# One inverse product a step in the chunked WKV recurrence

## What is computed

```python
def step(S, inp):
    r_t, w_t, k_t, v_t, kk_t, a_t = inp
    sa = jnp.einsum('bhvk,bhk->bhv', S, kk_t)
    S = (S * w_t[:, :, None, :]
         - sa[..., None] * (kk_t * a_t)[:, :, None, :]
         + v_t[..., None] * k_t[:, :, None, :])
    y = jnp.einsum('bhvk,bhk->bhv', S, r_t)
    return S, y
```

## Time and profile before

| | |
|---|---|
| runs, us | 2166.88, 2166.91, 2168.07, median 2166.91 |
| span of the profiled execution, us | 2162.8 |
| outside the span, against the median, us | 4.1 |
| PE busy in the span | 98% |
| DVE, ACT, POOL busy | 68%, 49%, 4% |
| recurrence, from step 0 to the first matmul of the next weight product | 1467.3 to 1563.9 us |
| mean use of the 16 DMA engines by the main queue | 55.8% |

### The profile page before, as it was taken

How to read it: one execution, slowest core, us unless ns; L and a number is a source line. 1 busy time by engine, 2 the same in 40 slices (tenths; PEclk the granted TensorE clock), 3 DMA queues, 4 the chain that set the end, 5 groups by cost and what they waited for, 6 DMA issues and landing times.

```text
span 2162.8 us, 36139 instructions
## 1 busy us (share of the span) xinstructions
PE 2128.1 (98%) x13990; PEld 1808.1 (84%) x13990; DVE 1466.9 (68%) x2083; ACT 1063.6 (49%) x1516; POOL 85.8 (4%) x75
## 2 busy tenths in 40 slices
PE   9999999999999999999899999999899999999998
PEld 7888878888888888888788888887788888888886
DVE  6556568885478855786795599884776544567656
ACT  5444455444444433444644766544434534456543
POOL 0800000000000000000000000001211000000000
PEclk9999999999999999999999999999999999999999
DMA  9654545555656556555465656653454555654553
GB/s 299 202 165 157 172 160 185 190 186 189 198 185 190 187 187 199 187 180 177 150 203 167 196 183 179 206 160 86 129 174 142 185 185 195 186 155 146 173 197 117
DMA packets 398856, 384.43 MB, mean 178 GB/s; under 512 B 43660, under 2 KB 395460, under 8 KB 397764
## 3 DMA queue, kind: packets, MB, share of 16 engines
q1 hardware_dynamic: 398728, 382.66, 55.8%
HBM read 375.73 MB, written 6.87 MB: 177 GB/s over the span
## 4 chain that ended last, share of the span: by engine, by line
PE 89%; DVE 7%; issue 2%; ACT 1%; DMA 1%; POOL 0%; SPq 0%; DVEq 0%; ACTq 0%; POOLq 0%
PE acc L894 35%; PE acc L897 17%; PE acc L1020 5%; PE acc L1022 5%; PE acc L1021 5%; PE acc L931 3%; PE acc L986 2%; PE acc L987 2%; PE acc L988 2%; PE aux L1319 2%; PE acc L934 1%; DVE w_lo L3001 1%; PE acc L1619 1%; PE acc L1620 1%; PE acc L1621 1%
## 5 line engine op out<-in xcount | busy, mean ns | idle before, releaser
L2448 DVE TENSOR_TENSOR w_lo<-raw_w,w_hi 128x1024 fp32r<-128x1024 f32 (+1 forms) x570 | 683.5, 1224 | 438.3 <-ACT w_hi L1692 437.5
L1692 ACT ACTIVATE w_hi<-raw_w 128x1024 fp32r<-128x1024 f32 (+1 forms) x570 | 586.3, 1045 | 706.0 <-PE acc L897 413.0
L894 PE MATMUL acc<-h,w_hi 128*128 128x512 f32 x1664 | 525.8, 397 | 0.0
L897 PEld LDWEIGHTS acc<-h,w_lo 128*128 128x128 f32 x1664 | 312.6, 188 | 73.8
L897 PE MATMUL acc<-h,w_lo 128*128 128x256 f32 x1664 | 327.0, 278 | 0.0
L894 PEld LDWEIGHTS acc<-h,w_hi 128*128 128x128 f32 x1664 | 254.7, 189 | 1.0
L894 PE MATMUL acc<-x_split,w_hi 128*128 128x512 f32 x704 | 225.1, 401 | 0.0
L894 PE MATMUL acc<-xs_b,w_hi 128*128 128x512 f32 x512 | 162.0, 398 | 1.0 <-DVE w_lo L3001 0.9
L897 PEld LDWEIGHTS acc<-x_split,w_lo 128*128 128x128 f32 x704 | 132.2, 188 | 31.2
L3001 DVE TENSOR_TENSOR w_lo<-raw_w,w_hi 128x1024 fp32r<-128x1024 f32 x96 | 116.8, 1219 | 42.1 <-ACT w_hi L2165 41.2
L894 PE MATMUL acc<-xs_a,w_hi 128*128 128x512 f32 x448 | 142.3, 399 | 0.7 <-DVE w_lo L3001 0.7
(11 more groups left out here) (459 smaller groups left out, 3223.5 us busy)
## 6 DMA issues: line engine op xcount, KB each, us to landing
raw_w<-in_w_up SPq DMA_DIRECT2D x172, 512.0 KB, 3.5
raw_w<-in_a_w_in SPq DMA_DIRECT2D x124, 512.0 KB, 3.9
raw_w<-in_w_in SPq DMA_DIRECT2D x64, 512.0 KB, 3.9
raw_w<-in_w_down SPq DMA_DIRECT2D x64, 512.0 KB, 3.5
raw_w<-in_b_w_qg SPq DMA_DIRECT2D x64, 512.0 KB, 3.7
raw_w<-in_w_o SPq DMA_DIRECT2D x32, 512.0 KB, 3.5
raw_w<-in_a_w_out SPq DMA_DIRECT2D x32, 512.0 KB, 3.5
raw_w<-in_w_k_shared SPq DMA_DIRECT2D x32, 512.0 KB, 3.3
```

The source lines that it names most:

```text
L894: pe.matmul(ACC[2 * b + f], WHI[:, q if hi is None else hi, k, f * P:(f + 1) * P], op[:, kt, :, :].rearrange("p h t -> p (h t)"), start=fi ...
L897: mm = pe.matmul(ACC[2 * b + f][:, 0:T], WLO[:, slot, k, f * P:(f + 1) * P], op[:, kt, 0, :], start=False, stop=last)
L1692: act.activation(WHI[:, u % 4, 0:ku, :], RAWW[:, u, 0:ku, :], ACT.Copy).then_inc(hi_made, 1)
L2448: dve.tensor_tensor(WLO[:, u, 0:ku, :], RAWW[:, u, 0:ku, :], WHI[:, u % 4, 0:ku, :].bitcast(F32), ALU.subtract)\
```

## The change

For all heads and chunks the corners are now made by PE in two blocks of 128 small products (32 x 32 tiles, 32 columns each), `corners_halfway` in step 0 and `corners` in step 1. For this:

- `t_scratch` becomes a full 64 x 64 layout. Two DMAs write zeros in its off-diagonal quarters (`blank_corners`, issued behind unit 88), two write the diagonal inverses. All four write runs of 32 values (128 bytes), 4096 runs each. 
- ACT turns the left diagonal inverses around (`left_turned`, behind unit 92), one DMA stores them, 8 DMAs of 1024 runs of 128 bytes load left and right factors, 4 load the cross blocks.
- ACT and DVE copy one half of each block of 128 products. SP stores the corners of groups 1 to 3 (3 DMAs of 1024 runs) and only then issues the bonus loads (`spread_bonus`, 2 MB), which before stood ahead of step 0.
- `load_t` is one DMA (512 runs of 256 bytes), plus the two cross loads in steps 0 to 3.

Steps 0 to 3 keep two inverse products. Steps 4 to 15 (`whole_step`) have one inverse product and no w product, no `US` copy and no add on DVE. Their order on PE is by tile shape: 64 x 64 (x_second, state times r, beta_pairs, u), then 128 x 64 (turn_k, turn_v, state product, y second term, turn_beta), then 64 x 64 (k_pairs of the step after next, x_first of the next). The state has two buffers (S and S_ODD), and y and state sums change banks from step to step. The core of the diff, with parts of SP's, PE's, ACT's and DVE's queues:

```diff
             def load_t(n):
                 g, c = STEPS[n]
                 m = n % 3
-                src = t_dram.rearrange("(f c h) b s t -> c h b s f t", c=NCH, h=2)
-                for hh in range(2):
-                    for b in range(2):
-                        at = 64 * hh + H * b
-                        sp.dma_start(TB[at:at + H, m, :, H * b:H * b + H], src[c, hh, b, :, 4 * g:4 * g + 4, :])\
-                          .then_inc(t_loaded[m], 16)
-                for e in range(2):
-                    sp.dma_start(CRS[64 * (1 - e):64 * (1 - e) + H, m, :, H:], cross_dram[g, c, e]).then_inc(t_loaded[m], 16)
+                src = t_dram.rearrange("(g i c h) s t -> g c (h s) i t", g=4, c=NCH, h=2)
+                sp.dma_start(TB[:, m, :, :], src[g, c]).then_inc(t_loaded[m], 16)
+                if n < WHOLE:
+                    for e in range(2):
+                        sp.dma_start(CRS[64 * (1 - e):64 * (1 - e) + H, m, :, H:], cross_dram[g, c, e]).then_inc(t_loaded[m], 16)
+
+            def blank_corners():
+                sp.wait_ge(blanked, 2)
+                for a, b in ((0, H), (H, 0)):
+                    sp.dma_start(t_dram[:, a:a + H, b:b + H], TB[:, 0, 0:1, 0:H].broadcast_to([P, H, H])).then_inc(t_stored, 16)
+
+            def load_left_and_right(g):
+                sp.dma_start(LEFT_ALL[H * g:H * g + H, :, :], left_dram[32 * g:32 * g + 32].rearrange("a r s -> r a s")).then_inc(inv_in, 16)
+                sp.dma_start(RIGHT_ALL[H * g:H * g + H, :, :], t_dram[32 * g:32 * g + 32, H:, H:].rearrange("a s t -> s a t")).then_inc(inv_in, 16)
+
+            def store_corners():
+                sp.wait_ge(blanked, 2 + 2 * CORNERS_COPIED)
+                for g in range(1, 4):
+                    sp.dma_start(t_dram[32 * g:32 * g + 32, 0:H, H:].rearrange("a s t -> s a t"), CORNERS[H * g:H * g + H, :, :])\
+                      .then_inc(bon_stored, 16)
...
             sp.wait_ge(inverted, 1)
-            sp.dma_start(t_dram, TT[:, :, :, :]).then_inc(t_stored, 16)
-            sp.wait_ge(blanked, 2)
-            sp.wait_ge(t_stored, 16)
-            for n in range(3):
-                load_t(n)
+            for b in range(2):
+                sp.dma_start(t_dram[:, H * b:H * b + H, H * b:H * b + H], TT[:, b, :, :]).then_inc(t_stored, 16)
+            for g in range(4):
+                sp.dma_start(CROSS_ALL[H * g:H * g + H, :, :].rearrange("s (b x) t -> s b (x t)", x=4), cross_dram[g].rearrange("c e s x t -> s (c e) (x t)")).then_inc(inv_in, 16)
+            sp.wait_ge(inverted, 2)
+            sp.dma_start(left_dram, OUTER[:, :].rearrange("p (r s) -> p r s", r=H)).then_inc(t_stored, 16)
+            sp.wait_ge(t_stored, ALL_STORED)
+            load_t(0)
+            for g in range(4):
+                load_left_and_right(g)
+            load_t(1)
+            load_t(2)
...
-            for g in range(4):
-                spread_bonus(g)
             for n in range(3, 4 * NCH):
                 sp.wait_ge(y_done, n - 2)
+                if n == WHOLE:
+                    sp.wait_ge(bon_stored, 64 + 48)
                 load_t(n)
+                if n == WHOLE - 1:
+                    store_corners()
+                    for g in range(4):
+                        spread_bonus(g)
...
+            def corner_products(lhs, rhs):
+                for a in range(H):
+                    for g in range(4):
+                        rows = slice(H * g, H * g + H)
+                        mm = pe.matmul(CORNER_BANKS[rows, a // 16, a % 16 * H:a % 16 * H + H], lhs(a)[rows], rhs[rows, a, :], start=True, stop=True)
+                mm.then_inc(corner_done, 1)
+
+            def corners_halfway():
+                pe.wait_ge(inv_in, CORNERS_IN)
+                pe.wait_ge(kb_out, 1)
+                corner_products(cross_of, LEFT_ALL)
+
+            def corners():
+                pe.wait_ge(blanked, 2 + CORNERS_COPIED)
+                pe.wait_ge(y_out, 1)
+                corner_products(lambda a: HALFWAY[:, a, :], RIGHT_ALL)
...
+            def whole_step(n):
                 g, c = STEPS[n]
                 more = n + 1 < len(STEPS)
                 state_next = more and STEPS[n + 1][1] < 3
                 if c > 0:
                     x_second(n)
+                    y_first(n)
                 if more:
+                    beta_pairs(n + 1)
+                pe.wait_ge(t_loaded[n % 3], t_count(n))
                 pe.wait_ge(xs_ready, n + 1)
+                u_product(n)
+                if state_next:
+                    turn_k(n + 1)
+                if c == 2:
+                    pe.wait_ge(gn_read, g)
                 if more:
                     turn_v(n + 1)
+                state_product(n)
+                y_second(n)
                 if state_next:
                     turn_beta(n + 1)
+                if c == 0:
+                    pe.wait_ge(vt_out, 2 * n + 4)
+                    group_squares(g - 1)
+                if n + 2 < len(STEPS):
+                    k_pairs(n + 2)
+                if more:
                     x_first(n + 1)
...
+            def left_turned():
+                act.wait_ge(inverted, 1)
+                act.activation(OUTER[:, :].rearrange("p (r s) -> p r s", r=H), TT[:, 0, :, :].rearrange("p s r -> p r s"), ACT.Copy).then_inc(inverted, 1)
...
+            def corner_copy(n):
+                act.wait_ge(corner_done, n + 1)
+                act.activation((HALFWAY, CORNERS)[n][:, 0:H // 2, :], CORNER_BANKS[:, 0, :].rearrange("p (a t) -> p a t", a=H // 2), ACT.Copy).then_inc(blanked, 1)
...
+                act.wait_ge(u_done, u_count(n))
                 act.activation(v_and_u(n % 2)[0:64, :, 1, :, :].rearrange("p j h t -> p h j t"), by_two(XU_BANKS[0:64, :, P:T]), ACT.Copy)\
                    .then_inc(us_ready, 1)
-                if n + 1 < len(STEPS):
+                if n >= WHOLE and more:
+                    v_copies(n + 1)
+                elif n >= WHOLE:
+                    operand_hi(0)
+                if n >= WHOLE and more:
+                    y_copy(n)
+                if more:
                     k_beta_copy(n + 1)
...
+                if n < 2:
+                    dve.wait_ge(corner_done, n + 1)
+                    dve.tensor_copy((HALFWAY, CORNERS)[n][:, H // 2:, :], CORNER_BANKS[:, 1, :].rearrange("p (a t) -> p a t", a=H // 2)).then_inc(blanked, 1)
...
+                if n + 1 >= WHOLE and n + 2 < len(STEPS):
+                    read_kappa(n + 2)
```

More of the change, by code:

```diff
@@ L1458, in step @@
             def step(n):
                 g, c = STEPS[n]
-                m = n % 2
+                state_next = STEPS[n + 1][1] < 3
+                if c > 0:
+                    x_second(n)
+                k_pairs(n + 1)
+                pe.wait_ge(t_loaded[n % 3], t_count(n))
+                pe.wait_ge(xs_ready, n + 1)
+                u_product(n)
+                turn_v(n + 1)
+                pe.wait_ge(us_ready, us_count(n) - 2)
+                quads(XU_BANKS, T, far(CRS[:, n % 3, :, :]), far(US), between, True, True).then_inc(w_done, 1)
@@ L1461, in step @@
+                state_product(n)
+                if state_next:
+                    turn_beta(n + 1)
+                if n + 1 < WHOLE:
+                    x_first(n + 1)
+                y_second(n)
+                if n + 1 == WHOLE:
+                    k_pairs(n + 2)
+                    x_first(n + 1)
+            def whole_step(n):
+                g, c = STEPS[n]
                 more = n + 1 < len(STEPS)
                 state_next = more and STEPS[n + 1][1] < 3
-                inverse, cross = block_of(TB[:, n % 3, :, :]), far(CRS[:, n % 3, :, :])
@@ L1464, in step @@
                 if c > 0:
                     x_second(n)
+                    y_first(n)
                 if more:
-                    k_pairs(n + 1)
-                pe.wait_ge(t_loaded[n % 3], 96 * (n // 3 + 1))
+                    beta_pairs(n + 1)
+                pe.wait_ge(t_loaded[n % 3], t_count(n))
                 pe.wait_ge(xs_ready, n + 1)
-                quads(XU_BANKS, P, inverse, mid(XS), across, True, True).then_inc(u_done, 1)
+                u_product(n)
+                if state_next:
+                    turn_k(n + 1)
@@ L1471, in step @@
+                if c == 2:
+                    pe.wait_ge(gn_read, g)
                 if more:
                     turn_v(n + 1)
-                pe.wait_ge(us_ready, 3 * n + 1)
-                quads(XU_BANKS, T, cross, far(US), between, True, True).then_inc(w_done, 1)
-                if c == 0 and g:
-                    group_squares(g - 1)
-                if more:
-                    beta_pairs(n + 1)
-                if n:
-                    pe.wait_ge(y_out, n)
-                if c > 0:
-                    quads(Y_BANKS, 0, state, at(R, n), channel, True, False).then_inc(s_read, 1)
@@ L1492, in step @@
-                if c == 3 and more:
-                    x_first(n + 1)
+                state_product(n)
+                y_second(n)
```

(29 more changed lines are left out.)

143 lines of the change are left out of this document (91 added, 52 removed).

## The result

| | before | after |
|---|---|---|
| runs, us | median 2166.89 (2163.95 to 2168.07, 4 runs) | median 2178.48 (2176.32 to 2180.99, 4 runs) |
| ratio after / before, 95% interval | | 1.0059 [1.0045, 1.0074] |
| span of the profiled execution, us | 2162.8 | 2174.7 |
| mean granted clock in it | 0.994 | 0.989 |

The forecast was 2161.3 with a range from 2158.4 to 2167.5.

The account below looks back on a forecast made before the run. PE was taken as close to full in the recurrence. Gain 13.4 late, less 0.7 and 0.6 in early steps, 6.0 for corners, 0.5 for factors: 5.6 us, from 2166.9 to 2161.3; range 2158.4 to 2167.5.

Parts of the forecast that it names:

- Late steps: Steps 4 to 15: fewer products and shape changes shorten PE's order, 69.9 to 55.5 us, a gain of 13.4 after 1.0 behind.
- The cover at step 14: Step 14: ACT makes two splits behind its copies and copies x for step 15 some 0.9 us late.
- the operand behind u(15): After the last u: DVE starts on the next product's operand 2.0 us behind it, before 1.0; 1.0 lost.
- DMAs ahead: Before the first corner block: small-run transfers finish in time, factors with 1 us of cover; 0.5 us charged.
- The two rivals that had PE waiting for factors: Ahead of the first block: factors late, 2 to 6 us (chance 0.18), or a large wait, from 10.4 us (0.09).
- the one with the long wait: Ahead of the first block: slow small runs or queue, PE waits 16.4 us at 34 ns a run, 2177.2; chance 0.09.
- Corner blocks: Steps 0 and 1: two blocks of 128 small products cost 3.0 us each, 6.0 together, range 2.2 to 4.2 a block.
- The rival that small products cost what larger ones do: Corner blocks: 32-column products cost what 64-column ones do; gain 3.2 us, 2163.7; chance 0.22.
- lies clear: Recurrence: corner stores and bonus loads are done by 1496, load_t(4) by 1497 for use near 1500; no cost charged.

Follow-up runs that it names:

- burst: Kernel before plus 256 unread products (32 x 32 tiles, 32 columns) in one go at unit 80 of the weight product ahead of the recurrence: 2177.49 us, 1.0055.
- cols: Kernel before plus 256 unread products of 32 x 32 tiles and 64 columns in one go at unit 80: 2175.3 us, 1.0048.
- spread: Kernel before plus 256 unread products (32 x 32 tiles, 32 columns), 16 at each of units 74 to 89: 2170.67 us, 1.0025.
- few: Kernel before plus 64 unread products of 32 x 32 tiles and 128 columns at unit 80: 2166.12 us, 1.0008.
- stagger: Changed kernel with bonus loads issued group by group with loads for steps 3, 5, 7, 11, and POOL's last bonus multiply after step 11: 2175.14 us, 1.0051.
- wide: Changed kernel with each block of 128 corner products replaced by 8 of 512 columns, which changes corner values: 2166.94 us, 1.0010.
- bonus_late: Kernel before with its 2 MB of bonus loads issued behind the loads for step 3 instead of ahead of step 0: 2168.8 us, 1.0011.

## Why the prediction was wrong

The forecast was a gain of 5.6 us in the span, the traces show a loss of 11.9. The 17.5 between them, in rounded parts: 11.0 in steps 0 and 1, 2.8 in steps 2 and 3, 2.7 in the late steps, 2.9 behind the recurrence, less 1.3 of lead at its start and 0.5 charged for the DMAs.

**Late steps: right in the mechanism.** Forecast from u(4) to u(15) 55.5, measured 58.15, before 69.9. The distances were 5.4, 4.85, 4.13 and 3.81 in steps 4 to 7 for a forecast of 5.6, 5.1, 4.1, 4.3. Luck is in the sum: these four were 0.9 under the forecast, and steps 8 to 11 well over it (6.12, 6.07, 7.26, 4.76), with 0.92 by issue within u(9) and the 2.08 for DVE at step 10, behind which the granted clock is 0.66 from 1545 to 1550. The cover at step 14, forecast at 0.9, was 1.21; the operand behind u(15), forecast 1.0 later, was 0.9 later.

**DMAs ahead: right.** The factors were in, and the first block began behind the w product with no wait; the last factor load was issued at 1463.81, and the right factors landed 3.7 to 4.0 us behind their issue, so all were in by 1467.8, 0.8 us ahead of the block, near the 1 us of cover forecast. The two rivals that had PE waiting for factors, 0.27 together, fall, though the one with the long wait named nearly the measured time (2177.2). A time alone doesn't confirm a mechanism.

**Corner blocks: the step that failed.** It took 3.0 us a block between bounds of 2.2 and 4.2, and said that "no row shows records held back by the issue". Measured: 6.6 us from the first block's start (1468.60) until beta_pairs gets going (1475.21), 6.5 for the second, and with the low clock behind them 8.7 and 8.9 more for steps 0 and 1. Forecast for the two steps were 6.6 (blocks and copies), measured 17.6. The array's own part was inside the bounds: 256 records took it 2.6 us (1.30 and 1.27), 10 ns each, and my reading of 15 ns a record was even high for it. What I left out is that a second limit stands beside the array: 256 instructions each 3.15 to 3.74 us (change and burst), 12 to 15 ns an instruction, 25 to 29 ns a record. Before, a step had 184 records, so 368 instructions in 6.12 us, 16.6 ns each: just slower than that limit. That nearly two blocks in reserve hid it is argued from the 246 records of the burst. The upper bound by records took the pace inside one call of 16 (15 ns); a step as a whole went at 33 ns a record, and no row showed a faster pace held over hundreds of records. The 0.88 by issue in the earlier trace rows, which I did not charge, was the sign of it: its packet of instructions comes 2.45 us ahead of PE, as in the blocks.

**The rival that small products cost what larger ones do** had the right direction and the wrong cause. `cols` shows that in a burst 64 columns cost the kernel what 32 do, but the array takes less for 32 (2.27 us for 246 records, 3.66 with 64), and `spread` and `few` show that the cost of a burst is no price of the product.

**What no case had:** two things. The bonus loads, 2 MB moved into the recurrence, of which I wrote that everything else "lies clear". Their data is not awaited (POOL's first multiply starts at 1511.13, right behind its squares of step 3), but they delay PE's instructions: 2.81 at step 3. And a bonus multiply met DVE's head pair in step 9, for which PE waited 2.08 in step 10. This is not by the loads: POOL has the multiply behind the squares of step 9 in both kernels, and before it came at 1530.29, when DVE's pair (1527.92) was done; in the shorter steps both come together. The rows of POOL and DVE after, then DVE in the staggered run, where the multiply is elsewhere:

```profile
1540.51 2.36 POOL L909 TENSOR_TENSOR bonus<-bonus,x 128x1024 f32<-128x1024 f32 x1
1540.88 2.67 DVE L3260 SCALAR_TENSOR_TENSOR beta<-beta,params,head_rstd_wide 128x256 f32<-128x256 f32 x2
```

```profile
1539.70 0.87 DVE L3261 SCALAR_TENSOR_TENSOR beta<-beta,params,head_rstd_wide 128x256 f32<-128x256 f32 x2
```

The pair takes 2.67 beside POOL and 0.87 alone. In `wide` it takes 2.67 beside the multiply too, and PE waits the same 2.08.

**The net.** Over 12 late steps the change saves 64 instructions a step, 768. It adds 1024 for 128 corners of two products each, of which a quarter serve nothing. At 12 to 15 ns each the 256 more would be 3 to 4 us, by my estimate, if the whole stretch ran at the pace of its instructions; no run shows that it does. The larger part of the loss is that the 1024 stand together, with the low clock behind them.

## What to carry over

Count PE's instructions, weight loads too, beside its array time: a float32 product is four. In the burst some 490 went at once and each further 256 took 3.74 us, so work that the array does faster than that, in a long row, pauses. Small products belong beside long ones (`spread`), or in fewer and wider calls (`wide`, `few`). Bulk loads beside a stretch dense in instructions can hold it up even if nobody waits for their data (`bonus_late`); spreading them moved the pauses and did not remove them (`stagger`).

## What was not expected of the hardware

- In a long row of small products, each 256 instructions of PE start 3.15 to 3.46 us apart with the data DMAs idle (DMA share 0.01), 3.74 in the burst and 4.01 with 64 columns. A pause there is shown only as "issue".
- Full DMA engines delay it: pauses of 2.57 to 3.42 us with no small products near, at a DMA share of 1.10 (bonus_late), 1.03 (the change, step 3) and 1.05 (wide).
- After the pauses of the blocks the granted clock is 0.50 for about 5 us, with PE busy again; so it is behind the 3.42 of `wide` (1496.7 to 1500), and it is 0.66 behind the 2.08 for DVE (1545 to 1550). Behind the single 2.81 of the change it stays 1.00 (1507 to 1510). `wide`, which has no pause in its blocks, has 0.992 in the mean against 0.989.
- A two-operation DVE pair on SBUF data went from 0.87 to 2.67 us beside a POOL multiply of 2.36 us.
